# The first query tile's softmax scaling on POOL, and every fourth head's probability copy on the vector engine, in two attention layers of a float32 transformer kernel

## What is computed

```python
# layer 0: one block, causal
lo = jnp.where((kpos[None, :] <= t[:, None])[None, :, None, :], lo, -jnp.inf)
probs = jax.nn.softmax(jnp.concatenate([lp, lo], axis=-1), axis=-1)
# layer 1: window of 128, with a sink
m = jnp.maximum(jnp.max(logits, axis=-1, keepdims=True), sink)
e = jnp.exp(logits - m)
probs = e / (jnp.sum(e, axis=-1, keepdims=True) + jnp.exp(sink - m))
# both
out = einsum(probs, v)
x = layer_norm(alpha * x + a.reshape(B, S, N_HEADS * HEAD_DIM) @ w_o[i], ...)
```

## Time and profile before

| | us |
|---|---|
| median of 3 runs | 2214.25 |
| lowest and highest run | 2213.52 and 2214.88 |
| the profiled execution | 2214.84 |
| its span on the core | 2213.0 |
| granted PE clock, mean | 0.999 |

### The profile page before, as it was taken

How to read it: one execution, slowest core, us unless ns; L and a number is a source line. 1 busy time by engine, 2 the same in 40 slices (tenths; PEclk the granted TensorE clock), 3 DMA queues, 4 the chain that set the end, 5 groups by cost and what they waited for, 6 DMA issues and landing times.

```text
span 2213.0 us, 30883 instructions
## 1 busy us (share of the span) xinstructions
PE 2171.3 (98%) x11392; PEld 1810.0 (82%) x11392; DVE 1730.2 (78%) x2006; ACT 1434.1 (65%) x1597; POOL 56.1 (3%) x72
## 2 busy tenths in 40 slices
PE   9999999999999999999999999999999999999998
PEld 6788897678888888888888887779978898987888
DVE  7665556688888898888888889867667886776886
ACT  6644444667777777777777777656565556565654
POOL 2000000020000000000000003000000000000000
PEclk9999999999999999999999999999999999999999
DMA  9755555269999999999999999843135454224451
GB/s 383 273 187 189 190 190 179 103 254 389 365 390 368 396 367 388 370 384 378 369 387 363 395 362 402 325 179 127 68 133 200 175 206 147 86 105 154 189 189 59
DMA packets 83235, 573.26 MB, mean 259 GB/s; under 512 B 9712, under 2 KB 10336, under 8 KB 17936
## 3 DMA queue, kind: packets, MB, share of 16 engines
q1 hardware_dynamic: 77472, 545.29, 64.7%
q0 software_dynamic: 5376, 26.12, 3.2%
q10 hardware_dynamic: 288, 0.52, 0.1%
HBM read 564.03 MB, written 17.83 MB: 263 GB/s over the span
## 4 chain that ended last, share of the span: by engine, by line
PE 88%; DVE 6%; ACT 4%; issue 2%; DMA 1%; SPq 0%; ACTq 0%; DVEq 0%
PE bank L810 64%; PE bank L876 10%; PE bank L878 5%; DVE w_lo L540 2%; ACT w_hi L535 2%; PE bank L1163 1%; PE bank L1288 1%; PE bank L1298 1%; DVE R L2051 1%; PE bank L1203 1%; DVE arena L2062 1%; ACT arena L1505 1%; DMA raw<-in_wu_qkv 1%; PE bank L779 1%; ACT L535 0%
## 5 line engine op out<-in xcount | busy, mean ns | idle before, releaser
L540 DVE TENSOR_TENSOR w_lo<-raw,w_hi 128x2048 fp32r<-128x2048 f32 x505 | 1155.5, 2299 | 262.4 <-ACT w_hi L535 260.8
L535 ACT CAST w_hi<-raw 128x2048 fp32r<-128x2048 f32 x505 | 963.4, 1911 | 343.3 <-PE bank L810 260.4
L810 PE MATMUL bank<-w_hi,xT 128*128 128x512 f32 x2368 | 754.1, 393 | 6.5 <-DVE w_lo L540 4.6
L810 PEld LDWEIGHTS bank<-w_hi,xT 128*128 128x128 f32 x2368 | 444.5, 188 | 113.5 <-DVE w_lo L540 13.5
L810 PE MATMUL bank<-w_lo,xT 128*128 128x512 f32 x1184 | 461.1, 389 | 0.0
L810 PE MATMUL bank<-w_hi,aT_hi 128*128 128x512 f32 x864 | 343.9, 398 | 1.0 <-DVE w_lo L540 1.0
L876 PE MATMUL bank<-xT,w_hi 128*128 128x512 f32 x960 | 340.3, 398 | 0.8 <-issue 0.4
L810 PE MATMUL bank<-w_hi,aT_lo 128*128 128x512 f32 x864 | 337.3, 390 | 0.0
L810 PE MATMUL bank<-w_lo,aT_hi 128*128 128x512 f32 x864 | 336.5, 390 | 0.0
L878 PE MATMUL bank<-xT,w_lo 128*128 128x256 f32 x960 | 269.5, 281 | 0.0
L810 PEld LDWEIGHTS bank<-w_lo,xT 128*128 128x128 f32 x1184 | 222.5, 188 | 44.2 <-issue 0.5
(11 more groups left out here) (346 smaller groups left out, 1717.0 us busy)
## 6 DMA issues: line engine op xcount, KB each, us to landing
raw<-in_wu_eg SPq DMA_DIRECT2D x112, 1024.0 KB, 7.2
raw<-in_wu_eu SPq DMA_DIRECT2D x112, 1024.0 KB, 7.1
raw<-in_wu_ed SPq DMA_DIRECT2D x112, 1024.0 KB, 7.2
raw<-in_wu_up SPq DMA_DIRECT2D x44, 1024.0 KB, 4.8
raw<-in_wu_ffn_gu SPq DMA_DIRECT2D x28, 1024.0 KB, 4.8
raw<-in_wu_in SPq DMA_DIRECT2D x28, 1024.0 KB, 4.9
raw<-in_wu_down SPq DMA_DIRECT2D x22, 1024.0 KB, 4.8
raw<-in_wu_ffn_d SPq DMA_DIRECT2D x14, 1024.0 KB, 4.8
```

The costliest lines, as they stand in the source:

```text
L535: nc.scalar.copy(w_hi[:, place(i), :], src).then_inc(*E.hi.mark("unit", i))
L540: nc.vector.tensor_tensor(w_lo[:, place(i), :], raw[:, i % RAW, :], w_hi[:, place(i), :].bitcast(F32), ALU.subtract) \
L810: mm = nc.tensor.matmul(o, l[i], r[j], start=(first and n == 0), stop=(last and n == 2), skip_group_check=not lone)
```

## The change

In layers 0 and 1, `normalise` on DVE makes the inverse and multiplies the second query tile only. POOL multiplies the first tile (128x256 for the two heads) for each of the eight pairs, released by the inverse; its mask load stands between pair 6 and pair 7, and the vector loads behind pair 7. PE's `turn_probs` waits for both multiplications. Of the odd pairs, ACT copies the first head's turned probabilities only; DVE copies the second head's, in the same step i, between scores(i) and normalise(i - 1), and waits there for the pair's transposes and for the values product of the pair before.

```diff
+        first_probs, inverted = ev.new("first_tile_probs"), ev.new("inverse_sums")
...
+            def first_tile(L, p):
+                a, c, at = TILES[0]
+                pr = att["pr"][:, p % 2, :, at:at + c - a]
+                gp.wait_ge(*inverted.at(L, p))
+                nc.gpsimd.tensor_tensor(pr, pr, rden[:, p % 2, :, 0:1].to_broadcast([P, 2, c - a]), ALU.mult) \
+                    .then_inc(*first_probs.mark(L, p))
+
             for L in range(2):
-                gp.wait_ge(*M.free[1].at("sc", L, 15))
-                load_mask(1 if L == 0 else 3)
+                for p in range(8):
+                    if p == 7:
+                        gp.wait_ge(*M.free[1].at("sc", L, 15))
+                        load_mask(1 if L == 0 else 3)
+                    first_tile(L, p)
                 load_vec(4 * L + 2)
...
             def turn_probs(L, p):
                 pe.wait_ge(*probs.at(L, p))
+                if L < 2:
+                    pe.wait_ge(*first_probs.at(L, p))
...
             def turned(L, p):
-                for e in range(2):
+                for e in range(1 if L < 2 and p % 2 else 2):
...
             def normalise(L, p):
                 i = p % 2
                 ve.wait_ge(*exped.at(L, p))
-                chain(V_.reciprocal(rden[:, i, :, :], rsum[:, i, :, :]))
-                for q, (a, c, at) in enumerate(TILES):
+                if L < 2:
+                    V_.reciprocal(rden[:, i, :, :], rsum[:, i, :, :]).then_inc(*inverted.mark(L, p))
+                    ve.wait_ge(*inverted.at(L, p))
+                else:
+                    chain(V_.reciprocal(rden[:, i, :, :], rsum[:, i, :, :]))
+                for q, (a, c, at) in list(enumerate(TILES))[L < 2:]:
...
+            def turned_late(L, p):
+                ve.wait_ge(*M.groups.at("pt", L, 2 * p + 1))
+                ve.wait_ge(*M.groups.at("pv", L, p - 1))
+                V_.tensor_copy(att["pt"][:, 1, :], bank[7][:, 0:384]).then_inc(*M.free[7].mark("pt", L, 2 * p + 1))
...
                 for i in range(2, 12):
                     if i < 8:
                         scores(L, i)
+                    if i < 10 and i % 2:
+                        turned_late(L, i - 2)
                     if i < 9:
                         normalise(L, i - 1)
```

## The result

The changed kernel takes 2222.16 us (median of 7 runs, 2221.04 to 2222.82), the kernel before 2214.25 (2213.04 to 2215.51): 7.91 us more, a ratio of 1.0033 with a 95% interval of 1.0023 to 1.0042. It is slower, and by more than the forecast's 2219.7, close to the upper end of the range.

A forecast was written before the change was run, and what follows sets the result against it. PE, busy 98%, loses time only in waits, in layers 0 and 1 through a latency loop of 5.74 us per two pairs. Delays of 2.42 + 3.02 = 5.4 us gave 2219.7; own range 2217.4 to 2222.3, with B 2214.2 to 2222.3.

The forecast's parts named there:

- The upper end: Of the forecast's own range, 2222.3: POOL's multiplication at 0.79 us and the copy at 0.60 give a sum of 8.0.
- POOL and DVE take turns: Attention, layers 0 and 1: DVE multiplies first, POOL follows for 0.64 us; PE starts 1.51 us after the inverse, not 1.30.
- Rival B: POOL and DVE run side by side; PE starts 0.13 us earlier than now; 2214.9 us; chance 0.16.
- Rival C: POOL gets in first and its 0.64 us hold DVE's multiplication too; at least 2221.1 us; chance 0.06.
- The rotation is held: DVE's rotation behind pair 0 waits for POOL, so pair 1's inverse moves by 0.30 us in both layers.
- The late copy: DVE's odd-pair copy waits for the previous values product, holding the next inverse; layer 0's loop 6.20 us instead of 5.74.
- over 1 us of idle for the first copy of a layer: Sign that the forecast is right: DVE idles that long, ended by PE's values product, ahead of each layer's first late copy.
- Layer 1's small copy waits for POOL: DVE's small copy ahead of its scores: if it waits, layer 1 loses 3.02 us (taken), if not, 2.20.
- The waits' sum: Delay of pair 6's transposes: 2.42 us in layer 0 plus 3.02 in layer 1, 5.4 on the span.
- Nothing behind absorbs the shift: Behind pair 6's transposes the work is PE's own, and layer 1's weight queue shifts along, so the delay reaches the span.
- At no cost: POOL's mask load ends before pair 7's inverse, and projection work in PE's queue covers a late pair 7.

The follow-up runs named there:

- products ahead of S6: Changed kernel plus two products nobody reads, in PE's idle ahead of pair 6's transposes; 2219.53 us.
- the copy behind the normalising: Changed kernel with DVE's late copy moved behind the next pair's inverse and multiplication instead of ahead of them; 2214.93 us.
- the copy with its own place: Changed kernel, but DVE's late copy writes its own buffer and waits only for its pair's transposes, not for the previous pair's values product; 2215.73 us.
- POOL behind DVE: Changed kernel, but POOL's multiplication is released by DVE's multiplication instead of the inverse, so the two can't overlap; 2221.86 us.
- the late copy alone: Changed kernel without POOL's part: DVE multiplies both query tiles again and still copies the second head of odd pairs; 2220.61 us.

## Why the prediction was nearly right, and for what it was short

The direction, the mechanism and the place were right, the sum was not: 5.4 us were forecast for the waits ahead of S6 and 4.4 were lost there, and a loss on PE's clock, 3.5 us by the profile, was not in it. That the measured time lay in the range is luck. The upper end had been set by dearer instructions, which did not come; without the clock the time would have been about 2214.25 + 4.4 = 2218.7 by the table, and 2219.53 was measured with products ahead of S6.

**POOL and DVE take turns: right.** In the changed kernel DVE's multiplication is as long as before (0.69) and POOL's ends 0.47 behind it; alone it takes 0.62, where 0.64 was taken. One term was wrong: POOL's start was put 0.30 behind its release, by its DMA issue. Its multiplication starts at 53.48, 0.08 after the inverse's record ends at 53.40, only 0.04 behind DVE's. DVE still came first in all 16 pairs. So PE starts at R + 1.47, not R + 1.51. *Rival B* would have shown POOL done within 1.15 us of R; it was done at R + 1.37. *Rival C* would have shown vector multiplications of over 1.2 us; they took 0.69, though C's condition, a start of POOL within 0.04 us, was much nearer than thought.

**The rotation is held: right, but its price was 0.08 and not 0.30.** Timeline of DVE:

```profile
46.10 0.18 DVE L2073 RECIPROCAL small<-small 128x4 f32<-128x4 f32 x1
46.31 0.69 DVE L2079 TENSOR_TENSOR arena<-arena,small 128x512 f32<-128x512 f32 x1
46.92 0.64 DVE L2038 TENSOR_TENSOR arena<-arena,small 128x64 f32<-128x64 f32 x1
47.48 0.21 DVE L2039 TENSOR_TENSOR arena<-arena,small 128x64 f32<-128x64 f32 x1
```

The first instruction takes 0.64 instead of 0.22 us and lets the next in at R + 1.38, when POOL's record ends. The prediction let the instruction begin only then; by the trace its own time lies inside the wait. R1 - R0 is 3.41, and was 3.33.

**The late copy: right, but for one sign.** R1 to R2 of layer 0 was bounded from below at 3.73 and measured 53.23 - 49.51 = 3.72; the loop was put at 6.20 and the even inverses are 6.20 and 6.19 apart (53.23, 59.43, 65.62). The copy takes 0.56 and lets the next step in after 0.47. That its wait in this place costs most, and not its length, was shown by the copy behind the normalising (+0.6 us) and by the copy with its own place (+1.6). The sign "over 1 us of idle for the first copy of a layer" held in layer 0 (1.24) and failed in layer 1: 0.31, and 0.51 with the products ahead of S6, where the clock was full; DVE comes later to its copy there.

**Layer 1's small copy waits for POOL: right.** The question was left open between +2.20 and +3.02. Timeline of DVE, layer 1, pairs 2 and 3:

```profile
415.05 0.17 DVE L2073 RECIPROCAL small<-small 128x4 f32<-128x4 f32 x1
415.25 0.69 DVE L2079 TENSOR_TENSOR arena<-arena,small 128x512 f32<-128x512 f32 x1
415.86 0.58 DVE L2059 COPY R<-small 128x4 f32<-128x4 f32 x1
416.36 0.34 DVE L2064 CUSTOM_DVE_ANT_0 R<-bank,msk,small 128x128 f32<-128x128 f32 x1
...
417.71 0.16 DVE L2073 RECIPROCAL small<-small 128x4 f32<-128x4 f32 x1
```

A copy of 128x4 that took 0.16 us takes 0.58 and lets the masking in at 416.36, R + 1.31. Where POOL starts after the copy, it is not held, as DVE's timeline with POOL behind DVE shows (POOL's record starts at 416.14):

```profile
415.98 0.16 DVE L2059 COPY R<-small 128x4 f32<-128x4 f32 x1
416.05 0.34 DVE L2064 CUSTOM_DVE_ANT_0 R<-bank,msk,small 128x128 f32<-128x128 f32 x1
```

The Trainium skill, page "SBUF — State Buffer", section "Who interferes with whom", says that copies in a two-port mode contend with GpSimd, and that whoever issues first holds the other for its whole instruction. The changed kernel's trace agrees, 0.58 us for the copy that came behind POOL's start; in the other trace the two do not overlap, and whether this copy ran in such a mode no run shows. As with the rotation, the copy's own time was put behind POOL's instead of into it: even to odd is 2.66 and not 2.88, the even inverses stand 6.38 us apart and not 6.6, and S6 moved by 2.30 without the slow clock behind S0.

**The waits' sum: 1.0 too high.** They came to 2.14 and 2.30 instead of 2.42 and 3.02. In layer 0 the held rotation was priced 0.22 too high and PE's start 0.04; in layer 1 the rotation 0.21, the small copy 0.23 in each of two turns, and PE's start 0.04.

**PE's clock: the term that was missing.** The prediction moved S6 and took all that PE does behind it as unchanged. It did see that PE would idle longer, and had the clock column at 1.00, and didn't ask whether a longer idle leaves it there. By the profile 1.56 + 1.51 + 0.39 = 3.5 us were lost to the clock, by the kernel with products ahead of S6 2.6. The 2.6 is the better price: it rests on medians, and the 0.39 behind S0 can't be laid to the change, since the clock fell there in other runs with the idle of the kernel before.

The run lists give a third figure, for the clock wherever it fell. The 31 runs of the kernel before in the first batch have mean granted clocks of 0.996 to 0.999: the fifteen at 0.999 have a median of 2213.65 us, the seven at 0.997 of 2215.53. All seven runs of the changed kernel are at 0.995 or 0.996. A thousandth of mean clock goes with 0.9 us in the first batch and 1.1 in the second (a straight line through 31 and 24 runs), and the mean of the changed kernel, 0.9959, lies 0.0023 below that of the kernel before, 0.9982: 2.1 to 2.5 us by this reading. It doesn't tell the place: the profiled execution with POOL behind DVE has a mean of 0.996 too, and its clock did not fall behind S6.

**Nothing behind absorbs the shift: right in sum.** S7 of layer 1 lies 435.27 - 428.49 = 6.78 us later, and the span is 7.3 longer: from that S7 to the end it takes 1785.0 us and took 1784.5.

**At no cost: right.** POOL's mask load and pair 7's late multiplication held nothing: S7 comes when the projection's first products end, in both layers.

Left open: why the clock fell where it did. Behind S6 it fell in both layers in the changed kernel, in one with the late copy alone, and in neither with POOL behind DVE, where the idle was longest. The length of the idle alone doesn't decide it, as S0 of layer 1 shows best. PE's timeline, first the kernel before, then the late copy alone (L943 and L944 are the eight transposes behind S0):

```profile
405.93 0.88 PE L923 MATMUL bank<-cst,arena 128*128 128x128 f32 x6 [1.86 <-DVE arena L2062]
406.64 1.04 PE L943 MATMUL bank<-cst,arena 128*128 128x128 f32 x8
```

```profile
406.77 1.24 PE L924 MATMUL bank<-cst,arena 128*128 128x128 f32 x6 [1.86 <-DVE arena L2067]
407.80 1.91 PE L944 MATMUL bank<-cst,arena 128*128 128x128 f32 x8
```

The idle is 1.86 us in both, and the clock fell behind one of them only. So the profiles, one execution each, don't show that the longer idle ahead of S6 alone brings the fall. What is shown is that with the idle filled the clock stayed and 2.6 us came back.

## What to carry to other kernels

A copy that is moved to a less loaded engine brings its waits along, and there they hold whatever stands behind it in that queue: put it behind the work that the next turn of the loop needs, or give it a place of its own. Splitting one elementwise step over DVE and POOL when both halves read two SBUF operands saved nothing here: the two took turns and ended 1.16 us after the first began, where DVE alone took 1.03, and DVE's next SBUF instruction paid too. And a stage's cost isn't only the delay of its end: where PE idles longer ahead of it, look at the granted clock behind it.

## What the runs showed of the hardware

- POOL's 128x256 multiplication takes 0.62 us alone and starts 0.08 us after the record of the DVE instruction that releases it ends, in the changed kernel (53.40 to 53.48) and with POOL behind DVE alike.
- While POOL multiplied, DVE instructions as short as 0.16 us were held too: a copy of 128x4 took 0.58, a 128x64 multiplication 0.64 instead of 0.22.
- The granted clock fell to the lower level behind idles of PE of 1.88 and 2.07 us and stayed at the higher one behind 1.89 and 2.29; behind idles of 1.86 at one place of the program it did both.
